# Value products of two quads of heads issued together in the attention stage of a two-layer decoder trunk

## The chip, the cores and the metric

The kernel runs on one core of a Trainium2 chip, in one launch. The metric is device time in microseconds (us); less is better. The kernel before took 1133.11 us, the median of three runs (1133.06 to 1133.26). One further execution was taken with the hardware profiler; all rows shown here come from it.

## The reference

Two layers of a hybrid decoder are computed for one sequence of 512 tokens with 1024 features, in float32. Layer 0 mixes tokens by a gated linear recurrence beside a short gated convolution; layer 1 mixes them by sliding-window attention. Each layer then has a mixture of 16 experts (two of one group for each token) and a gated per-layer embedding. The part that this case is about is the attention of layer 1: 16 query heads of width 64 over 2 key/value heads, a window of 128 keys, a learned sink for each head.

```
s = einsum('bnqkgd,bnskd->bkgnqs', q, kk) * scale        # scores, 128 queries x 256 keys for a block and head
s = where(mask, s, -inf)                                  # band of 128 keys
m = maximum(max(s, axis=-1), sink)
e = exp(s - m)
probs = e / (sum(e, axis=-1) + exp(sink - m))
o = einsum('bkgnqs,bnskd->bnqkgd', probs, vv)             # the value products
return o.reshape(bsz, t, D_MODEL) @ w_out + b_out
```

Everything else (the recurrence, the experts, the norms) is computed before and after this and is the same in both kernels.

## The kernel before

The program is written by hand, engine by engine, in one block for each engine; each engine works through its own list in order, and semaphores join them. There is no scheduler: the order in the code is the order on the chip. Large matrix products split each float32 operand into a high and a low part and take three products (`dense`). ScalarE (ACT) makes the high parts (`whi`, `ahi`), VectorE (DVE) the low ones (`wlo`, `alo`).

Attention is worked through in 16 quads. A quad is four heads of one block of 128 queries: quad w belongs to query block w // 4. For a quad the steps are these.

- `score(w)`, TensorE (PE): four matmuls of 64 rows each into the PSUM banks 4 and 5 (even quads) or 6 and 7 (odd quads). It raises `t_s`. In the profile these are the matmuls `psum<-arena` of shape 64*128.
- `mask_max(w, j)`, DVE, L2653 and L2659: a small copy and four mask-and-maximum instructions. Each of the four raises `t_neg`.
- `probs(u)`, ACT, L1870: four exponentials (u counts half quads, 0 to 31). Each raises `t_e`.
- `normalise(w)`, DVE, L2669 and L2672: one reciprocal and four scalings. Each scaling raises `t_prob`.
- `prob_T(u)`, PE, L1306: four transposes for a half quad into PSUM bank 2 or 3. It raises `t_pT`.
- `pT_copy(u)`, ACT, in the profile L1383 `arena<-psum`: a copy of the transposed probabilities out of PSUM. It raises `t_pTc`. The copies of a quad go to one of two buffers (`probs_T(w)`, chosen by w % 2), so from quad 2 on the copy waits for the value products of two quads earlier.
- `values(w)`, PE: four matmuls (two for quads 0 to 3, whose first key block is empty) into half of PSUM bank 0 or 1. It raises `t_pv`. In the profile these are the matmuls `psum<-arena` of shape 128*64.
- `o_hi(hb)`, ACT, L1383 `ahi<-psum`, and `o_lo(hb)`, DVE, L2678: the two parts of the output of two quads (hb = w // 2), after both their value products. `o_lo` raises `t_lo`.

The profile shows each float32 matmul of these steps as two records, so a quad's scores are x8 and its value products x8 (x4 for quads 0 to 3). The line of all matmuls that go through the helper is L569.

The waits that matter for the copy are written in ACT's block:

```
def pT_copy(u):
    w, j = u // 2, u % 2
    act.wait_ge(t_pT, u + 2)
    if w >= 2:
        act.wait_ge(t_pv, w - 1)
```

The order in the main loop, w from 0 to 15, is: on PE `prob_T(2w)`, `prob_T(2w + 1)`, `score(w + 3)`, `values(w - 1)`; on ACT `probs` of quad w + 1, `pT_copy(2w)`, `pT_copy(2w + 1)`, and in odd turns from 3 on `o_hi(w // 2 - 1)`; on DVE `mask_max` of quad w + 2, `normalise(w + 1)`, and in odd turns from 3 on `o_lo(w // 2 - 1)`. A "turn w" below is one pass of this loop, and "copy 2w" is `pT_copy(2w)`. After the loop come the value products of quad 15 and the output projection, a `dense` of 128x512 matmuls on PE, whose weights were loaded earlier.

Of the kernel before, what the change touches and what calls it, by code (L numbers as in the profile page):

```python
# [134 lines left out]
def build(nc, gm0, consts, hconsts, aconsts, gains, bout, x, pT, w_dense, w_moe, w_proj, out,  # L135
# [6 lines left out]
    with ctx:  # L142
# [237 lines left out]
        def first_key(n):  # L380

            return P if n == 0 else 0
# [5 lines left out]
        def probs_T(w):  # L388

            return area(AR_PTT, 2, 2, 512)[:, w % 2]  # L390
# [176 lines left out]
        def _(pe):  # L567
            def mm(o, l, r, start, stop, **kw):
                return nc.tensor.matmul(o, l, r, start=start, stop=stop, **kw)  # L569
# [686 lines left out]
            for q in range(2):  # L1256
                bank_read(BLK["akv"], q)
                o = PS[q][:, :]
                for kt in range(KT):
                    w = slice(kt * 256 + q * P, kt * 256 + (q + 1) * P)  # L1260
# [20 lines left out]
            def score(w):  # L1281


                n = w // 4
                if w < 4:
                    pe.wait_ge(t_q, (5, 5, 7, 9)[w])
                if w >= 2:
                    pe.wait_ge(t_neg, 4 * (w - 1))
                for j in range(2):
                    for hh in range(2):  # L1290
                        r = slice(64 * hh, 64 * hh + 64)
                        o = PS[4 + w % 2 * 2 + hh]
                        last = mm(o[:, j * KEYS + first_key(n):(j + 1) * KEYS],
                                  QT[r, 2 * (w % 4) + j, n * P:(n + 1) * P],
                                  KTa[r, n * P + first_key(n):(n + 2) * P], True, True)
                last.then_inc(t_s, 1)

            def prob_T(u):
                w, j = u // 2, u % 2
                pe.wait_ge(t_prob, 2 * u + 2)  # L1300
                if u >= 2:
                    pe.wait_ge(t_pTc, u - 1)
                for hh in range(2):
                    for kb in range(first_key(w // 4) // P, 2):
                        at = (hh * 2 + kb) * P
                        last = nc.tensor.transpose(  # L1306
                            PS[2 + j][:, at:at + P],
                            soft(w)[:, 2 * j + hh, kb * P:(kb + 1) * P], ident)
                last.then_inc(t_pT, 1)

            def values(w):


                n, hb = w // 4, w // 2
                pe.wait_ge(t_pTc, 2 * w + 2)
                if w % 2 == 0 and hb >= 2:
                    pe.wait_ge(t_lo, hb - 1)
                first = first_key(n) // P
                o = PS[hb % 2][:, w % 2 * 256:(w % 2 + 1) * 256]
                for kb in range(first, 2):  # L1320
                    for hh in range(2):
                        r = slice(64 * hh, 64 * hh + 64)
                        at = (hh * 2 + kb) * P
                        last = mm(o[r, :].rearrange("p (a b) -> p a b", a=2),
                                  VN[:, n + kb, hh * HD:(hh + 1) * HD],
                                  probs_T(w)[:, :, at:at + P], kb == first, kb == 1)
                last.then_inc(t_pv, 1)
# [12 lines left out]
            for w in range(QUADS):  # L1340
                prob_T(2 * w)
                prob_T(2 * w + 1)
                if w + 3 < QUADS:
                    score(w + 3)
                if w >= 1:
                    values(w - 1)
            values(QUADS - 1)

# [1570 lines left out]
```

## Time and profile before

| what | value |
|---|---|
| median of three runs | 1133.11 us |
| the profiled execution, its own time | 1134.14 us |
| its span in the profile | 1131.9 us |
| PE busy | 1107.4 us (98%) |
| DVE busy | 894.3 us (79%) |
| ACT busy | 749.9 us (66%) |
| mean granted TensorE clock | 0.998 of full speed |
| attention loop | about 663.5 to 710.2 us of the span |

The span is the time from the first to the last instruction in the profile; the execution's own time is 2.24 us longer, and this execution took 1.03 us more than the median. Busy time is a union of an engine's instructions. A row of the timeline gives the start, the length, the engine, the line and the operation with its operands; in square brackets stands the idle time before it, where there is one, and who ended it. Groups of equal instructions are merged into one row with a count.

### The profile page before, as it was taken

To read this page: it belongs to the slowest core of one execution; us is meant where nothing else is said; L and a number is where in the kernel's file an instruction comes from. 1 tells how busy PE (TensorE), PEld (TensorE's weight loads), DVE (VectorE), ACT (ScalarE), POOL (GpSimd) and SP (SyncE) were. 2 spreads that over 40 slices of the span, in tenths; PEclk is the share of its full clock that TensorE was granted. 3 is DMA by queue.
4 is the path that set the end of the run, shared out by engine and by line. 5 is a ranking of instruction groups with operands and counts; after the bars stand their busy time and mean duration, and the time that the engine had idled before them with its cause. 6 is when DMAs were issued, how large, how long until landed. Compare 5 with 4: busy or idle time off the path is not lost.

```text
span 1131.9 us, 16852 instructions
## 1 busy us (share of the span) xinstructions
PE 1107.4 (98%) x5722; PEld 886.0 (78%) x5722; DVE 894.3 (79%) x1226; ACT 749.9 (66%) x957; POOL 131.2 (12%) x91
## 2 busy tenths in 40 slices
PE   9999999999999999999999999999999999999996
PEld 7888878757888888888788866776888888888785
DVE  6483777368999999998966479637999999999886
ACT  7483322347878787788565469436787878787765
POOL 0000000011212212120000000001221212221000
PEclk9999999999999999999999999999999999999999
DMA  9473213336999999998851210433999999999632
GB/s 368 171 279 149 94 47 135 154 120 245 358 390 372 383 372 386 377 377 348 324 202 44 106 38 20 168 112 138 339 366 384 377 386 373 391 371 382 262 136 75
DMA packets 50595, 286.28 MB, mean 253 GB/s; under 512 B 9321, under 2 KB 9597, under 8 KB 21358
## 3 DMA queue, kind: packets, MB, share of 16 engines
q1 hardware_dynamic: 37086, 250.93, 57.6%
q0 software_dynamic: 13456, 34.65, 8.3%
q8 instruction: 33, 0.54, 0.2%
q14 instruction: 20, 0.16, 0.0%
HBM read 271.38 MB, written 30.41 MB: 267 GB/s over the span
## 4 chain that ended last, share of the span: by engine, by line
PE 86%; DVE 7%; ACT 4%; issue 1%; DMA 1%; ACTq 0%; DVEq 0%; POOLq 0%
PE psum L569 81%; PE psum L938 2%; DVE arena L2659 2%; ACT whi L1383 2%; DMA arena<-vscr,cur 1%; DVE arena L2672 1%; PE psum L979 1%; DVE wlo L1942 1%; PE psum L849 1%; ACT ahi L1383 1%; DVE h L2493 0%; DVE h L2500 0%; DVE wlo L1938 0%; DVE h L2486 0%; PE psum L655 0%
## 5 line engine op out<-in xcount | busy, mean ns | idle before, releaser
L1938 DVE TENSOR_TENSOR wlo<-raw,whi 128x2048 fp32r<-128x2048 f32 x200 | 456.1, 2289 | 69.8 <-ACT whi L1383 59.5
L569 PE MATMUL psum<-whi,ahi 128*128 128x512 f32 x1088 | 433.6, 400 | 2.7 <-ACT ahi L1383 2.1
L569 PE MATMUL psum<-wlo,ahi 128*128 128x512 f32 x1088 | 422.8, 390 | 0.8 <-DVE wlo L1942 0.8
L569 PE MATMUL psum<-whi,alo 128*128 128x512 f32 x1088 | 418.3, 391 | 0.0
L1383 ACT ACTIVATE whi<-raw 128x2048 fp32r<-128x2048 f32 x200 | 382.8, 1916 | 41.7 <-PE psum L569 41.7
L569 PEld LDWEIGHTS psum<-whi,ahi 128*128 128x128 f32 x1088 | 204.3, 188 | 49.2 <-issue 4.5
L569 PEld LDWEIGHTS psum<-whi,alo 128*128 128x128 f32 x1088 | 204.2, 188 | 43.7
L569 PEld LDWEIGHTS psum<-wlo,ahi 128*128 128x128 f32 x1088 | 204.5, 188 | 40.0 <-DVE wlo L1942 1.2
L1383 ACT ACTIVATE arena<-psum 128x512 f32<-128x512 f32 (+3 forms) x150 | 83.3, 565 | 109.0 <-PE psum L569 77.9
L1383 ACT ACTIVATE ahi<-psum 128x512 fp32r<-128x512 f32 x146 | 81.8, 594 | 102.8 <-PE psum L938 39.3
L2767 POOL DMA_INDIRECT arena<-vscr,cur x32 | 69.5, 2172 | 386.1 <-DVE cur L2379 370.9
L569 PE MATMUL psum<-ahi,whi 128*128 128x512 f32 x240 | 95.4, 398 | 1.1 <-DVE wlo L1942 1.1
L569 PE MATMUL psum<-ahi,wlo 128*128 128x512 f32 x240 | 93.6, 390 | 0.0
L569 PE MATMUL psum<-alo,whi 128*128 128x512 f32 x240 | 93.5, 389 | 0.0
L569 PE MATMUL psum<-arena 128*64 128x256 f32 (+10 forms) x762 | 89.0, 319 | 0.9 <-ACT arena L1383 0.8
L569 PEld LDWEIGHTS psum<-arena 128*128 128x128 f32 (+5 forms) x762 | 54.7, 151 | 29.0 <-issue 15.6
L2775 POOL DMA_INDIRECT yscr<-arena,cur x30 | 45.0, 1500 | 89.1 <-ACT arena L1383 86.3
L569 PEld LDWEIGHTS psum<-ahi,whi 128*128 128x128 f32 x240 | 45.1, 188 | 11.7 <-DVE wlo L1942 1.6
L569 PEld LDWEIGHTS psum<-ahi,wlo 128*128 128x128 f32 x240 | 45.0, 188 | 9.6
L569 PEld LDWEIGHTS psum<-alo,whi 128*128 128x128 f32 x240 | 45.1, 188 | 9.2 <-issue 0.2
L1942 DVE SCALAR_TENSOR_TENSOR wlo<-raw,arena,whi 128x512 fp32r<-128x512 f32 x48 | 32.8, 745 | 17.9 <-ACT whi L1383 17.8
L2394 DVE TENSOR_TENSOR alo<-psum,ahi 128x512 fp32r<-128x512 f32 x64 | 40.9, 679 | 3.9 <-ACT ahi L1383 3.9
(222 smaller groups left out, 894.5 us busy)
## 6 DMA issues: line engine op xcount, KB each, us to landing
raw<-w_moe_dram SPq DMA_DIRECT2D x192, 1024.0 KB, 8.8
raw<-w_dense_dram SPq DMA_DIRECT2D x34, 1024.0 KB, 8.8
yscr<-arena POOLq DMA_DIRECT2D x2, 4096.0 KB, 24.3
arena<-yscr SPq DMA_DIRECT2D x6, 1024.0 KB, 6.8
vscr<-arena POOLq DMA_DIRECT2D x8, 512.0 KB, 2.9
h<-x_dram SPq DMA_DIRECT2D x4, 512.0 KB, 7.5
arena<-w_proj_dram POOLq DMA_DIRECT2D x2, 1024.0 KB, 6.9
arena<-yscr SPq DMA_DIRECT2D x4, 512.0 KB, 4.4
```

What stands on the lines that cost most here:

```text
L569: return nc.tensor.matmul(o, l, r, start=start, stop=stop, **kw)
L849: last = nc.tensor.transpose(PS[4 + half][:, t * P:(t + 1) * P], h[:, tb, kt * P:(kt + 1) * P], ident)
L938: last = nc.tensor.transpose(PS[4 + half][:, t * P:(t + 1) * P], area(AR_XGS[par], D)[:, kt * P:(kt + 1) * P], ident)
L979: last = nc.tensor.transpose(PS[6][:, t * P:(t + 1) * P], area(AR_HID, 512)[:, t * P:(t + 1) * P], ident)
L1383: return nc.scalar.activation(o, i, ACT.Copy, scale=scale)
L1938: tt(wlo[:, b % SPL, :], raw[:, b % RAW, :], halves(whi[:, b % SPL, :]), ALU.subtract).then_inc(lo_ready, 1)
L1942: last = stt(wlo[:, b % SPL, w], raw[:, b % RAW, w], g, halves(whi[:, b % SPL, w]), ALU.mult, ALU.subtract)
L2394: tt(alo[w], PS[4 + half][:, :].rearrange("p (a b) -> p a b", a=4), halves(ahi[w]), ALU.subtract).then_inc(m["xlo"], 1)
L2659: nc.vector.tensor_tensor_reduce(out=soft(w)[:, 2 * j + hh, a:KEYS], in0=PS[4 + w % 2 * 2 + hh][:, j * KEYS + a:(j + 1) * KEYS], in1=mk[:, ...
L2672: ts(pr, pr, rden[:, k:k + 1], None, ALU.mult).then_inc(t_prob, 1)
L2767: nc.gpsimd.indirect_dma_start(out=area(AR_XGS[par], D), out_offset=None, in_=vscr[layer], in_offset=bass.IndirectOffsetOnAxis(ap=cur[:, p ...
L2775: nc.gpsimd.indirect_dma_start(out=yscr[layer], out_offset=bass.IndirectOffsetOnAxis(ap=cur[:, 2 + par:3 + par], axis=0), in_=area(AR_OUTS ...
```

## The change

In the PE loop, the value products are no longer issued in each turn. In an odd turn w the products of quad w - 2 and of quad w - 1 are issued one behind the other, behind the scores of quad w + 3. In an even turn none are issued. In turn 1 only quad 0 is there. ACT's, DVE's and all other lists stay as they are, and so do all waits.

```
                 prob_T(2 * w + 1)
                 if w + 3 < QUADS:
                     score(w + 3)
-                if w >= 1:
+                if w % 2 == 1:
+                    if w >= 2:
+                        values(w - 2)
                     values(w - 1)
             values(QUADS - 1)
```

The order on PE in the turns 6 and 7, before. L1306 are the transposes, L569 128x256 the scores, L569 64x256 the value products; the first eight rows that are no transposes belong, two by two, to the scores of quad 9, the values of quad 5, the scores of quad 10 and the values of quad 6.

```order
L569 MATMUL psum<-arena 128x256 [waits t_neg]
L569 MATMUL psum<-arena 128x256 x3
L569 MATMUL psum<-arena 64x256 [waits t_pTc]
L569 MATMUL psum<-arena 64x256 x3
L1306 MATMUL psum<-con,arena 128x128 [waits t_pTc,t_prob]
L1306 MATMUL psum<-con,arena 128x128 x3
L1306 MATMUL psum<-con,arena 128x128 [waits t_pTc,t_prob]
L1306 MATMUL psum<-con,arena 128x128 x3
L569 MATMUL psum<-arena 128x256 [waits t_neg]
L569 MATMUL psum<-arena 128x256 x3
L569 MATMUL psum<-arena 64x256 [waits t_lo,t_pTc]
L569 MATMUL psum<-arena 64x256 x3
```

The same place in the changed kernel, from the scores of quad 9 on:

```order
L569 MATMUL psum<-arena 128x256 [waits t_neg]
L569 MATMUL psum<-arena 128x256 x3
L1306 MATMUL psum<-con,arena 128x128 [waits t_pTc,t_prob]
L1306 MATMUL psum<-con,arena 128x128 x3
L1306 MATMUL psum<-con,arena 128x128 [waits t_pTc,t_prob]
L1306 MATMUL psum<-con,arena 128x128 x3
L569 MATMUL psum<-arena 128x256 [waits t_neg]
L569 MATMUL psum<-arena 128x256 x3
L569 MATMUL psum<-arena 64x256 [waits t_pTc]
L569 MATMUL psum<-arena 64x256 x3
L569 MATMUL psum<-arena 64x256 [waits t_lo,t_pTc]
L569 MATMUL psum<-arena 64x256 x3
```

The values of quad 5 have moved behind the transposes of quad 7 and the scores of quad 10.

The second place is the end of the loop on PE, turn 15, before. The rows are the transposes of quad 15, the values of quads 14 and 15, and the first matmul of the output projection.

```order
L1306 MATMUL psum<-con,arena 128x128 [waits t_pTc,t_prob]
L1306 MATMUL psum<-con,arena 128x128 x3
L1306 MATMUL psum<-con,arena 128x128 [waits t_pTc,t_prob]
L1306 MATMUL psum<-con,arena 128x128 x3
L569 MATMUL psum<-arena 64x256 [waits t_lo,t_pTc]
L569 MATMUL psum<-arena 64x256 x3
L569 MATMUL psum<-arena 64x256 [waits t_pTc]
L569 MATMUL psum<-arena 64x256 x3
L569 MATMUL psum<-whi,ahi 128x512 [waits t_pTc,t_lo,lo_ready]
```

And in the changed kernel, from the second half of these transposes on:

```order
L1306 MATMUL psum<-con,arena 128x128 [waits t_pTc,t_prob]
L1306 MATMUL psum<-con,arena 128x128 x3
L569 MATMUL psum<-arena 64x256 [waits t_pTc]
L569 MATMUL psum<-arena 64x256 x3
L569 MATMUL psum<-arena 64x256 [waits t_lo,t_pTc]
L569 MATMUL psum<-arena 64x256 x3
L569 MATMUL psum<-arena 64x256 [waits t_pTc]
L569 MATMUL psum<-arena 64x256 x3
L569 MATMUL psum<-whi,ahi 128x512 [waits t_pTc,t_lo,lo_ready]
```

The values of quad 13 now stand behind all transposes of quad 15, with those of quads 14 and 15 behind them.

## Rows read from the trace of the kernel before

**Rows 1.** Busy time of PE, PEld, DVE, ACT, POOL; then PEclk, DMA share, GB/s.

```profile
684.19:690.69 6.50, 6.36 (x52) 4.04 (x50) 6.43 (x32) 6.50 (x22) 0.00 (x0) 1.00 0.00 0
```

**Rows 2.** Chain of waits: start, us, engine and line.

```profile
699.57 1.61 DVE arena L2659 x8
...
708.43 23.88 PE psum L569 x112
```

**Rows 3.** Waits of PE in the loop: us in total, times, longest.

```profile
PEld psum L1306 <- DVE arena L2672: 8.8, 15, 1.2
```

**Rows 4.** Timeline of turns 9 to 12: DVE, PE and ACT.

```profile
692.31 0.68 DVE L2678 TENSOR_TENSOR alo<-psum,ahi 128x512 fp32r<-128x512 f32 x1
...
692.98 0.47 DVE L2659 CUSTOM_DVE_ANT_0 arena<-psum,arena 128x256 f32<-128x256 f32 x1
...
694.80 1.14 DVE L2672 TENSOR_SCALAR arena<-arena 128x256 f32<-128x256 f32 x4
...
695.48 1.18 PE L1306 MATMUL psum<-con,arena 128*128 128x128 f32 x8
...
696.17 1.12 ACT L1383 ACTIVATE arena<-psum 128x512 f32<-128x512 f32 x2
...
696.59 2.15 PE L569 MATMUL psum<-arena 64*128 64x256 f32 x16
...
697.19 0.59 ACT L1383 ACTIVATE ahi<-psum 128x512 fp32r<-128x512 f32 x1
...
699.64 1.07 ACT L1383 ACTIVATE arena<-psum 128x512 f32<-128x512 f32 x2
```

**Rows 5.** Timeline: turn 3, and the copies of turns 5, 7 and 9.

```profile
670.20 0.66 ACT L1383 ACTIVATE arena<-psum 128x256 f32<-128x256 f32 x2
...
670.36 1.72 PE L569 MATMUL psum<-arena 64*128 64x256 f32 x12
...
670.75 0.59 ACT L1383 ACTIVATE ahi<-psum 128x512 fp32r<-128x512 f32 x1
...
676.67 1.12 ACT L1383 ACTIVATE arena<-psum 128x512 f32<-128x512 f32 x2 [0.43 <-PE psum L1306]
...
683.17 1.12 ACT L1383 ACTIVATE arena<-psum 128x512 f32<-128x512 f32 x2
...
689.67 1.12 ACT L1383 ACTIVATE arena<-psum 128x512 f32<-128x512 f32 x2
```

**Rows 6.** Timeline from turn 13 to the output projection.

```profile
702.76 1.12 ACT L1383 ACTIVATE arena<-psum 128x512 f32<-128x512 f32 x2
...
703.17 1.08 PE L569 MATMUL psum<-arena 128*64 128x256 f32 x8
...
703.78 0.59 ACT L1383 ACTIVATE ahi<-psum 128x512 fp32r<-128x512 f32 x1
...
707.25 1.18 PE L1306 MATMUL psum<-con,arena 128*128 128x128 f32 x8
...
707.94 1.12 ACT L1383 ACTIVATE arena<-psum 128x512 f32<-128x512 f32 x2 [0.65 <-PE psum L1306]
...
708.36 1.95 PE L569 MATMUL psum<-arena 128*64 128x256 f32 x16
...
710.24 0.50 PE L569 MATMUL psum<-whi,ahi 128*128 128x512 f32 x1
...
710.36 0.60 ACT L1383 ACTIVATE ahi<-psum 128x512 fp32r<-128x512 f32 x1 [0.80 <-PE psum L569]
...
710.99 0.69 DVE L2678 TENSOR_TENSOR alo<-psum,ahi 128x512 fp32r<-128x512 f32 x1 [0.71 <-ACT ahi L1383]
```

**Rows 7.** Weight load in turn 11 behind the scores; columns as in rows 4.

```profile
697.65 0.63 PEld L569 LDWEIGHTS psum<-arena 128*64 128x64 f32 x8 [0.33 <-ACT arena L1383]
```

**Rows 8.** Busy time by engine and granted clock at the program's end; columns as in rows 1.

```profile
1122.00:1126.00 4.00, 1.18 (x6) 0.64 (x4) 1.93 (x5) 3.82 (x5) 0.00 (x0) 1.00 0.94 349
1126.00:1131.00 5.00, 0.00 (x0) 0.00 (x0) 2.21 (x5) 1.67 (x4) 0.00 (x0) 0.57 0.37 141
```

More of the change, by code:

```diff
@@ L1344, in _ @@
                     score(w + 3)
-                if w >= 1:
+                if w % 2 == 1:
+                    if w >= 2:
+                        values(w - 2)
                     values(w - 1)
```

## The prediction

> **What bounds the kernel now.** PE is busy 98% of the whole span, but the change touches one stage, so I read that stage. First the chain of waits: inside the attention loop it does not run over PE. It steps from DVE group to DVE group, and only from 708.43 on is it PE again, with the output projection [rows 2]. Then the busy time of one pair of turns (an even and an odd one), a stretch of 6.50 us between two `o_hi`: ACT is busy 6.50 of 6.50 us, DVE 6.43, PE 6.36, and the DMA share is 0.00 [rows 1]. So ACT and DVE have no slack, and a pair of turns costs 6.50 us because ACT's list is that long. PE's 6.36 us overstate it: its weight loads for the transposes wait 15 times for DVE's scalings, 8.8 us in all [rows 3]. PE works in the gaps the other two leave. What the reader is to see: a delay of ACT or DVE in this loop costs its full length, a change in PE's work costs only what it makes them wait.
>
> Last the timeline of one odd turn, 11 [rows 4]. DVE's scalings start at 694.80, the transposes at 695.48, ACT's first copy at 696.17, before the scores at 696.59 begin. The copy needs the products of quad 9 too (`t_pv`), but these were issued in turn 10, long before, so this wait costs nothing today.
>
> **The change part by part.** No instruction is added or removed; all 16 calls of `values` are moved or stay. Moved are those of the odd quads 1, 3, ..., 13: each goes from an even turn to the next odd one, behind eight transposes and the scores. Seven copies wait for exactly these products: copy 2w with w = 3, 5, ..., 15 waits for quad w - 2. Behind each of these copies ACT has its partner copy, `o_hi` and then the next exponentials, and DVE's `o_lo` waits for `o_hi`. No DMA is issued in this loop by SP or in PE's list, no queue is passed, and the even quads keep their place or stand 1 us later behind their partner, where only `o_hi` needs them (it stands behind two copies of 1.12 us that wait longer).
>
> What the wait costs the first time: in turn 3 the scores of quad 6 start at 670.36 with the products behind them, together x12 and 1.72 us, which is what would stand there now too (eight score records, four of a short quad) [rows 5]. The products end at 672.08. From a product's end to ACT it takes 0.05 us: 708.36 + 1.95 = 710.31 against `o_hi` at 710.36 [rows 6]. So copy 6 starts at 672.13 instead of 670.20 [rows 5]: 1.93 us late.
>
> From there a loop closes that was not closed before, and its length sets the pace. From one waiting copy to the next:
> 1. copy to `o_hi`: 697.19 - 696.17 = 1.02 [rows 4]; in turn 3 the copies are short, 670.75 - 670.20 = 0.55 [rows 5]
> 2. `o_hi` to `o_lo`: 710.99 - 710.36 = 0.63 [rows 6]
> 3. `o_lo` to the masks of the next quad: 692.98 - 692.31 = 0.67 [rows 4]
> 4. masks to scalings: 694.80 - 692.98 = 1.82 [rows 4]
> 5. scalings to transposes: 695.48 - 694.80 = 0.68 [rows 4]
> 6. transposes to scores: 696.59 - 695.48 = 1.11 [rows 4]
> 7. scores and the products behind them, to the release: 2.15 + 0.05 = 2.20 [rows 4]; with a short quad behind them 1.72 + 0.05 = 1.77 [rows 5]; without scores 1.08 + 0.05 = 1.13 [rows 6]
>
> Sum: 1.02 + 0.63 + 0.67 + 1.82 + 0.68 + 1.11 + 2.20 = 8.13 us for a pair, against 6.50. Each full pair adds 1.63 us. The scalings also need ACT's four exponentials, which stand between `o_hi` and the next copies: 699.64 - 697.19 = 2.45 us for `o_hi` and these four [rows 4]. They are ready 1.02 + 2.45 = 3.5 us behind the waiting copy, and the scalings come at 1.02 + 0.63 + 0.67 + 1.82 = 4.14. They fit.
>
> Now turn by turn, the start of the waiting copy, new against old:
> - turn 3: 672.13 against 670.20, +1.93
> - turn 5: 0.55 + 0.63 + 0.67 + 1.82 + 0.68 + 1.11 + 1.77 = 7.23 on, 679.36 against 676.67, +2.69 [rows 5]
> - turn 7: 8.13 on, 687.49 against 683.17, +4.32 [rows 5]
> - turn 9: 695.62 against 689.67, +5.95 [rows 5]
> - turn 11: 703.75 against 696.17, +7.58 [rows 4]
> - turn 13: no scores are left, 8.13 - 2.20 + 1.13 = 7.06 on, 710.81 against 702.76, +8.05 [rows 6]
> - turn 15: no masks are left. 1.02 to `o_hi`, then 707.25 - 703.78 = 3.47 to the transposes (over the last exponentials), 708.36 - 707.25 = 1.11, and 1.13 for the products of quad 13: 6.73 on, 717.54 against 707.94, +9.60 [rows 6]
>
> The end: the products of quad 15 need the second copy, 717.54 + 1.12 = 718.66. By then PE is done with quad 14 (two products take 1.95 us, from 716.41 to 718.36). From the start of the last products to the output projection it is 1.88 / 2 = 0.94, where 1.88 = 710.24 - 708.36 [rows 6]. So the projection starts near 719.6 instead of 710.24: +9.4 us.
>
> Behind it everything moves as one piece. The DMA queues stand still in the loop (share 0.00 [rows 1]), the weights of the next stages are in their buffers, and loads resume when these are used; nothing there is nearer to the loop's old end than to its new one. On the profiled execution this gives 1131.9 + 9.4 = 1141.3 us of span and 1134.14 + 9.4 = 1143.5 us of time. The profiled execution lay 1.03 us over the median of the runs, so a median of **1142.5 us** is predicted.
>
> Bounds of what the trace does not show. A product that ACT waits for behind scores is shown nowhere: from below it comes 697.65 - 696.59 = 1.06 (scores) [rows 4, 7] plus 0.94 (one of two products) [rows 6] = 2.00 behind the scores' start, from above at 2.15 + 0.63 (step 2, the longest such hand-over here); I take 2.20, next to the observed end of the products. The lower end takes 0.2 off six times, the upper adds 0.6 six times: -1.2 and +3.5 us. Steps 1 to 6 were seen with engines that were full; each may be 0.05 us off, over some 35 steps that is 1.7 us either way. If the even turn's copies or the second half's transposes have some slack that my chain charges, the turns 13 and 15 lose most, up to 2 us.
>
> **A rule of the Trainium skill.** In turn 11 the weight load of the products has 0.33 us before it behind the scores [rows 7], which I take as the price of a change of matmul kind. "TensorEngine Tiling (Array Packing)" of the Trainium skill, section "Key Properties", says that a change of the tiling mode drains TensorE; by it scores (64*128), products (128*64) and transposes (128*128) each cost a drain, and the change has five switches in a pair of turns instead of six. By that rule alone the time would fall; the size and what it is worth are the second rival below.
>
> **The rivals.**
>
> *The late products cost once, not in each pair.* If ACT or DVE could catch up between two waits, only the last turn would count: transposes at 707.25, products of quad 13 until 709.49, copy at 709.49 instead of 707.94, +1.55; a chain that catches up half of each pair's 1.63 gives 1.93 + 0.76 + 3 x 0.82 + 0.24 + 0.78 = 6.2 less the 0.2 at the end. Times: 1134.7 to 1139. Against it speaks that ACT is busy 6.50 of 6.50 and DVE 6.43 [rows 1]. For it, that DVE sat only on part of the chain's waits and rounding may hide 0.1 us here and there.
>
> *PE's switches are the bound (faster).* Where PE's issue of three kinds of matmul sets the pace, one gap of 0.33 us goes in each of seven even turns: 7 x 0.33 = 2.3 us, 1130.8 us. It decides as soon as PE does not wait for DVE before its transposes. Against it: PE's loads do wait there, 15 times, 8.8 us [rows 3], over 0.5 us each time; a gap of 0.33 us taken out only lengthens that wait. This is the side of a gain, and it needs the copies not to wait for the moved products, which the code excludes.
>
> *Every wait adds in full.* If the transposes kept their distance from ACT's list and not from DVE's, each of seven copies would come 696.59 + 2.20 - 696.17 = 2.62 us late on top of a full ACT: 7 x 2.5 = 17.5 us, 1150.6 us. Against it: the transposes hang on the scalings, and these on masks and exponentials that begin before the wait ends.
>
> *The clock falls.* With pairs of 8.13 us PE is busy 6.36 / 8.13 = 78%. If the granted clock went to 1.2 GHz there, steps 6 and 7 (3.3 us) would take twice as long, five to six times: 17 to 20 us more, about 1161 us. The trace speaks against it: the clock is 1.00 (2.4 GHz) even in 4 us with 1.18 us of PE work, and falls to 0.57 only where PE does nothing for 5 us [rows 8].
>
> **How the numbers follow.** What this kernel's measurement can tell from no change is about 0.2%, 2.3 us. Chances: the closed loop as worked out 76% (own range 1140 to 1145); catching up, 12%, of which a third stays under +2.3 us; full addition 5%; the clock 2%; PE's switches 2%; nothing measurable for another reason 3%. Slower is then 76 + 8 + 5 + 2 = 91%, the same 4 + 3 = 7%, faster 2%. The likeliest is 1142.5. For 8 in 10 the closed loop is taken with the upper part of the catching up: 1139 to 1145.5.
>
> **What the changed kernel's profile would show.** ACT's row for the copies in the odd turns gets idle time before it, released by PE's L569 and not by L1306: about 1.6 us in each full pair, some 11 us in all with the ends. DVE's `o_lo` (L2678) waits for `ahi` in each odd turn, where it now does so only twice. The pair of turns is 8.1 us long in the middle of the loop, PE's matmul counts are the same, the clock stays at 1.00, and behind the output projection all stages keep their lengths. If the pair stays at 6.5 us, step 7 or the reading that ACT is full is wrong. If it is 9 us, the exponentials and not `o_lo` carry the chain. If the loop is 8.1 us and the total is not up by nine, something behind it gives time back.

## The result and the profile after

The changed kernel takes 1147.75 us, the median of four runs (1146.49 to 1149.23), against 1133.18 us for the kernel before: a ratio of 1.0127 with a 95% interval of 1.0113 to 1.0142, 14.6 us slower. The prediction said 1142.5 us and a range up to 1145.5: slower was right, the size was not. The four runs also spread over 2.7 us, where the kernel before spreads over 0.3 in four runs (over 1.3 and 1.8 us in the fifteen and twenty runs taken of it for the experiments). The clock in their records goes with it: 0.995 at 1146.49 us, 0.994 at 1147.33, 0.992 at 1148.17 and 1149.23.

The page of the profile shows the first sign in section 2. Part 1 and the granted clock by slices:

```profile
span 1145.1 us, 16852 instructions
...
PE 1110.5 (97%) x5722; PEld 888.0 (78%) x5722; DVE 895.2 (78%) x1226; ACT 749.8 (65%) x957; POOL 131.6 (11%) x91
...
PEclk9999999999999999999999998999999999999999
```

The counts are those of before. The busy time of ACT and DVE is within 1 us of before; PE's has grown by 3.1 us with the same instructions, and one slice has an 8 in the clock row, where the kernel before had a 9.

The waits of the stretch 660 to 722 us (us in total, times, longest), where before the transposes' loads waited 8.8 us [rows 3]:

```profile
PEld psum L1306 <- DVE arena L2674: 16.0, 11, 2.3
ACT arena L1385 <- PE psum L569: 15.1, 7, 3.7
PE psum L1306 <- DVE arena L2674: 11.9, 8, 1.9
DVE alo L2680 <- ACT ahi L1385: 9.2, 6, 3.1
```

The second row is the predicted wait: seven copies on ACT wait for PE's L569, the products, and the fourth is DVE's `o_lo` behind them. Predicted were some 11 us for the copies, not 15.1.

The timeline at the same places as [rows 4 to 6], ACT's waiting copies of the turns 3, 5, 7, 9, 11, 13 and 15, with PE and DVE in turn 7 and PE's transposes and first projection matmul later on:

```profile
671.98 0.66 ACT L1385 ACTIVATE arena<-psum 128x256 f32<-128x256 f32 x2 [1.90 <-PE psum L569]
...
679.27 1.09 ACT L1385 ACTIVATE arena<-psum 128x512 f32<-128x512 f32 x2 [1.26 <-PE psum L569]
...
684.05 1.18 PE L1306 MATMUL psum<-con,arena 128*128 128x128 f32 x8 [1.86 <-DVE arena L2674]
...
685.16 3.01 PE L569 MATMUL psum<-arena 64*128 64x256 f32 x24
...
687.41 1.09 ACT L1385 ACTIVATE arena<-psum 128x512 f32<-128x512 f32 x2 [1.69 <-PE psum L569]
...
689.02 0.69 DVE L2680 TENSOR_TENSOR alo<-psum,ahi 128x512 fp32r<-128x512 f32 x1 [1.55 <-ACT ahi L1385]
...
695.57 1.09 ACT L1385 ACTIVATE arena<-psum 128x512 f32<-128x512 f32 x2 [1.70 <-PE psum L569]
...
700.35 1.64 PE L1306 MATMUL psum<-con,arena 128*128 128x128 f32 x8 [1.86 <-DVE arena L2674]
...
705.28 1.09 ACT L1385 ACTIVATE arena<-psum 128x512 f32<-128x512 f32 x2 [3.25 <-PE psum L569]
...
713.26 1.08 ACT L1385 ACTIVATE arena<-psum 128x512 f32<-128x512 f32 x2 [1.52 <-PE psum L569]
...
717.70 1.78 PE L1306 MATMUL psum<-con,arena 128*128 128x128 f32 x8 [1.92 <-DVE arena L2674]
...
721.49 1.08 ACT L1385 ACTIVATE arena<-psum 128x512 f32<-128x512 f32 x2 [3.74 <-PE psum L569]
...
723.64 0.50 PE L569 MATMUL psum<-whi,ahi 128*128 128x512 f32 x1
```

The loop begins 0.21 us earlier in this span than in that of before (the first transposes stand at 663.35 and not 663.56), so 0.21 is added for a comparison. Turn 5 then has its copy at 679.48 (predicted 679.36), turn 7 at 687.62 (687.49), turn 9 at 695.78 (695.62). A pair is 687.41 - 679.27 = 8.14 and 695.57 - 687.41 = 8.16 us long; 8.13 was predicted. Up to here the forecast holds to 0.2 us. The next pair is 705.28 - 695.57 = 9.71 us. Its transposes start as far behind the last copy as before (4.78 us), but last 1.64 instead of 1.18, and the copy waits 3.25 instead of 1.70. The same stretch by engines, with three more (columns as in [rows 1]):

```profile
690.00:692.00 2.00, 0.34 (x4) 0.00 (x0) 1.97 (x11) 2.00 (x7) 0.00 (x0) 1.00 0.00 0
...
700.00:704.00 4.00, 3.65 (x18) 2.40 (x20) 3.73 (x18) 2.02 (x9) 0.00 (x0) 0.61 0.00 0
...
710.00:714.00 4.00, 3.94 (x22) 2.53 (x24) 3.45 (x17) 2.48 (x10) 0.00 (x0) 0.64 0.33 129
...
718.00:722.00 4.00, 4.00 (x24) 2.60 (x22) 0.17 (x1) 0.51 (x2) 0.00 (x0) 0.58 0.00 0
```

The column behind POOL's is the granted clock, as a mean over the row: 1.00 is 2.4 GHz, and a value such as 0.61 is a stretch that ran partly at 2.4 and partly at 1.2 GHz. The clock fell three times, each time within 1.1 us after PE had taken up its work again behind a gap like that of the first row, and it was still down when ACT came to wait for PE. The gap of the first row itself was followed by no fall. The projection starts at 723.85 instead of 710.24, 13.6 us late, of which 9.4 were predicted. Behind it nothing changes: the step into the experts waits for the same DMA at 809.75 instead of 796.35, with the 0.21 again 13.6 us later. From profiled run to profiled run the times differ by 1147.33 - 1134.14 = 13.2 us; the medians differ by 1.4 more, since the profiled execution of before was 1.0 slower than its median and that of the changed kernel 0.4 faster.

### The profile page after: what moved, and what is told of

It reads as the page before. It is cut to its first block, busy times and chain, and to the rows that moved or that the text cites. A ratio compares the mean times of both kernels' runs of the same rounds, so it can differ in the third digit from the quotient of the medians.

```text
span 1145.1 us, 16852 instructions
## 1 busy us (share of the span) xinstructions
PE 1110.5 (97%) x5722; PEld 888.0 (78%) x5722; DVE 895.2 (78%) x1226; ACT 749.8 (65%) x957; POOL 131.6 (11%) x91
## 4 chain that ended last, share of the span: by engine, by line
PE 86%; DVE 6%; ACT 4%; DMA 2%; issue 2%; SPq 0%; ACTq 0%; DVEq 0%; POOLq 0%
PE psum L569 80%; PE psum L938 2%; DMA arena<-vscr,cur 1%; ACT whi L1385 1%; PE psum L979 1%; DVE arena L2661 1%; ACT ahi L1385 1%; PE psum L1306 1%; DVE wlo L1944 1%; DMA h<-x_dram 1%; ACT arena L1385 1%; PE psum L849 1%; DVE h L2495 0%; DVE arena L2674 0%; DVE h L2502 0%
## 5 line engine op out<-in xcount | busy, mean ns | idle before, releaser
L569 PE MATMUL psum<-whi,ahi 128*128 128x512 f32 x1088 | 433.5, 400 | 2.6 <-ACT ahi L1385 2.1
L569 PE MATMUL psum<-wlo,ahi 128*128 128x512 f32 x1088 | 422.9, 390 | 0.8 <-DVE wlo L1944 0.8
L569 PE MATMUL psum<-whi,alo 128*128 128x512 f32 x1088 | 418.2, 391 | 0.0
L569 PEld LDWEIGHTS psum<-whi,ahi 128*128 128x128 f32 x1088 | 204.3, 188 | 49.2 <-issue 4.4
L569 PEld LDWEIGHTS psum<-whi,alo 128*128 128x128 f32 x1088 | 204.2, 188 | 43.6
L569 PEld LDWEIGHTS psum<-wlo,ahi 128*128 128x128 f32 x1088 | 204.5, 188 | 40.3 <-DVE wlo L1944 1.2
L569 PE MATMUL psum<-ahi,whi 128*128 128x512 f32 x240 | 95.4, 398 | 1.1 <-DVE wlo L1944 1.1
L569 PE MATMUL psum<-ahi,wlo 128*128 128x512 f32 x240 | 93.6, 390 | 0.0
L569 PE MATMUL psum<-alo,whi 128*128 128x512 f32 x240 | 93.5, 390 | 0.0
L569 PE MATMUL psum<-arena 32*128 32x128 f32 (+10 forms) x762 | 91.7, 329 | 1.3 <-ACT arena L1385 1.1
L569 PEld LDWEIGHTS psum<-arena 128*128 128x128 f32 (+5 forms) x762 | 57.0, 156 | 30.4 <-issue 18.7
L569 PEld LDWEIGHTS psum<-ahi,whi 128*128 128x128 f32 x240 | 45.0, 188 | 11.7 <-DVE wlo L1944 1.6
L569 PEld LDWEIGHTS psum<-ahi,wlo 128*128 128x128 f32 x240 | 45.1, 188 | 9.5
L569 PEld LDWEIGHTS psum<-alo,whi 128*128 128x128 f32 x240 | 45.1, 188 | 9.2 <-issue 0.2
```

## The experiments

Theory A: the loop over the late products costs the 9.4 us worked out, and the rest is the granted clock, which fell because PE stood still for 1.9 us in each pair. Theory B: the rest lies in other waits of the loop. Each run is timed beside the kernel before on its own chip; that took 1133.93 us in the first four and 1133.55 us in the last four.

**PE's gap filled.** The changed kernel, with the scores of the odd quads 5 to 15 computed twice (`EXTRA = 4`), and as many spare matmuls in turn 14.

```
+EXTRA = 4
...
-                for j in range(2):
-                    for hh in range(2):
+                extra = EXTRA if w % 2 == 1 and w >= 5 else 0
+                pairs = [(j, hh) for j in range(2) for hh in range(2)]
+                for j, hh in pairs + pairs[:extra]:
+                    if True:
...
+                if w == 14:
+                    pe.wait_ge(t_neg, 4 * QUADS)
+                    for i in range(EXTRA):
+                        mm(PS[6 + i % 2][:, 0:KEYS], QT[0:64, 0, 0:P],
+                           KTa[0:64, 0:KEYS], True, True)
```

> The changed kernel with extra work for PE where it idles: the scores of the odd quads 5 to 15 (issued in even turns) are computed twice, into the same place with the same result, and four matmuls into unused PSUM stand at the end of turn 14. Each fills 1.06 us of the 1.9 us in which PE waits for the scalings. Theory (the closed loop costs 9.4 us, and the other 5 us are the granted clock, which fell because PE stood still for 1.9 us in each pair): the pair of turns stays at 8.15 us, the clock stays at 1.00, the time is 1142.5 us (1141.5 to 1143.5) and its spread is under 0.5 us. Rival (the 5 us lie in the loop's own waits or behind the loop): the time stays near 1147.7 us whatever the clock does, or rises by the added 6.4 us of PE work.

Measured: 1143.53 us (1143.00 to 1143.98), 9.6 us over before, ratio 1.0085 (1.0070 to 1.0100). With more work for PE the kernel took 4.2 us less than the changed kernel's 1147.75 us, and 5.0 us less when each is set against the kernel before as timed beside it (9.6 against 14.6 us). The spread is 1.0 us, not under 0.5. ACT's copies of the turns 9 to 15, the projection, and the clock where it had fallen:

```profile
695.44 1.09 ACT L1393 ACTIVATE arena<-psum 128x512 f32<-128x512 f32 x2 [1.69 <-PE psum L570]
...
703.59 1.09 ACT L1393 ACTIVATE arena<-psum 128x512 f32<-128x512 f32 x2 [1.69 <-PE psum L570]
...
710.67 1.08 ACT L1393 ACTIVATE arena<-psum 128x512 f32<-128x512 f32 x2 [0.63 <-PE psum L570]
...
717.41 1.09 ACT L1393 ACTIVATE arena<-psum 128x512 f32<-128x512 f32 x2 [2.24 <-PE psum L570]
...
719.56 0.50 PE L570 MATMUL psum<-whi,ahi 128*128 128x512 f32 x1
```

```profile
700.00:704.00 4.00, 3.78 (x32) 2.59 (x32) 3.61 (x17) 2.31 (x9) 0.00 (x0) 1.00 0.02 4
...
710.00:714.00 4.00, 4.00 (x29) 2.89 (x26) 2.45 (x10) 3.37 (x12) 0.00 (x0) 1.00 0.21 85
```

The steps are 8.15, 7.08, 6.74 and 2.15 us; predicted were 8.13, 7.06, 6.73 and 2.06. In the changed kernel they were 9.71, 7.98, 8.23 and 2.15: the three falls of the clock cost 1.56 + 0.90 + 1.49 = 3.95 us in the profiled run. PE's longest wait before transposes is 1.0 us here, against 1.9. Theory A holds, and B is out: ACT's waits and the pair of 8.15 us are as they were while the clock was up, and only the falls are gone. Filling the gap makes it shorter and PE busier at once, so the run does not tell which of the two kept the clock up.

**Half of the filling** (`EXTRA = 2`).

> As fill4, with half of the extra work: two more matmuls (0.53 us) in each even turn from 2 on, PE's wait is left at 1.3 us in each pair. Theory: the pair stays at 8.15 us; the clock is steadier than in the changed kernel, 1142.5 us if 1.3 us of standing still is short enough, something up to 1146 us if not. Rival: 1147.7 us as before, since half the idle time is still there.

Measured: 1144.07 us (1143.05 to 1144.13), 10.1 us over before, ratio 1.0086 (1.0070 to 1.0101). In the profiled run PE stood still for 1.26 and then four times for 1.42 or 1.43 us before the transposes (not the 1.3 expected), with the clock at 1.00 behind all five. It fell behind the next gap, that of turn 15:

```profile
714.95 1.18 PE L1309 MATMUL psum<-con,arena 128*128 128x128 f32 x8 [1.52 <-DVE arena L2682]
```

```profile
716.00:718.00 2.00, 2.00 (x12) 1.19 (x12) 0.00 (x0) 0.00 (x0) 0.00 (x0) 0.55 0.00 0
```

The last two steps are 7.54 and 2.44 instead of 6.74 and 2.15: a fall worth 1.1 us. Half of the filling keeps most of the clock.

**The products of two quads ahead of the scores.**

```
                 prob_T(2 * w + 1)
-                if w + 3 < QUADS:
-                    score(w + 3)
                 if w % 2 == 1:
                     if w >= 2:
                         values(w - 2)
                     values(w - 1)
+                if w + 3 < QUADS:
+                    score(w + 3)
```

> The value products of two quads still go together in odd turns, but ahead of the scores of quad w + 3 and not behind them. Theory of the closed loop: the release comes 1.13 us behind the transposes and not 2.20, the loop is 8.13 - 1.07 = 7.06 us against ACT's own 6.50; by turns the copies are late by about 0.8, 0.8, 1.3, 1.9, 2.5, 2.9, 4.4 us, the projection by 4.3 us: 1137.4 us (1136.5 to 1138.5), clock 1.00 since PE's wait shrinks to about 1 us. Rival (grouping itself costs, by drains or by the copies of two quads that collide, and not the place behind the scores): near 1142 us or more, as in the changed kernel.

Measured: 1139.76 us (1139.10 to 1141.30), 5.8 us over before, ratio 1.0053 (1.0038 to 1.0069). The waiting copies of the turns 7 and 9, PE's transposes of turn 15 and the projection:

```profile
685.48 1.08 ACT L1385 ACTIVATE arena<-psum 128x512 f32<-128x512 f32 x2 [0.63 <-PE psum L569]
...
692.56 1.08 ACT L1385 ACTIVATE arena<-psum 128x512 f32<-128x512 f32 x2 [0.63 <-PE psum L569]
...
711.17 1.18 PE L1306 MATMUL psum<-con,arena 128*128 128x128 f32 x8 [2.58 <-DVE arena L2674]
...
715.62 0.50 PE L569 MATMUL psum<-whi,ahi 128*128 128x512 f32 x1
```

The pair is 7.08 us (7.06 expected) and the projection 4.9 us late (4.3 expected; the loop begins 0.47 later in this span, which is taken off). The total missed by 1.5 us, of which 0.6 is in the loop's ends; the other 0.9 stays open, though in the profiled run 0.47 of it stand ahead of the loop, where the order is the same. The clock was 1.00 in the profiled run's loop, also behind the gap of 2.58 us; the run at 1141.30 had a clock of 0.995. The grouping is the same here as in the changed kernel, and the price is 5.8 us instead of 9.6 (with the clock up in both): the place behind the scores costs the other 3.8. What is left I put down to the place behind the transposes of turn w, for which the copy still waits; no run tries it alone.

**One late product.** The order of before, with quad 7's products in turn 9 (`LATE = (9,)`).

```
+LATE = (9,)
...
-                if w >= 1:
+                if w in LATE:
+                    values(w - 2)
+                if w >= 1 and w + 1 not in LATE:
+                    values(w - 1)
```

> The order of the kernel before in all turns but one: the products of quad 7 go from turn 8 to turn 9, behind the scores of quad 12. The copy of turn 9 then starts at 690.09 + 2.20 = 692.29 instead of 689.67, 2.6 us late. Theory: ACT is full, so a single late copy is never caught up: 1133.2 + 2.6 = 1135.8 us (1135.3 to 1136.2). Rival (a single wait is caught up, in part or in full, since only the loop over DVE, 1.63 us a pair, is truly on the path): 1134.8 us or less, down to 1133.2.

Measured: 1135.70 us (1135.35 to 1137.08), 1.8 us over before, ratio 1.0016 (1.0007 to 1.0025). ACT's copies of the turns 9, 11, 13 and 15:

```profile
693.01 1.09 ACT L1386 ACTIVATE arena<-psum 128x512 f32<-128x512 f32 x2 [2.68 <-PE psum L570]
...
699.36 1.07 ACT L1386 ACTIVATE arena<-psum 128x512 f32<-128x512 f32 x2
...
705.69 1.08 ACT L1386 ACTIVATE arena<-psum 128x512 f32<-128x512 f32 x2
...
710.84 1.12 ACT L1386 ACTIVATE arena<-psum 128x512 f32<-128x512 f32 x2 [0.65 <-PE psum L1307]
```

The copy comes 2.68 us late, as expected (the loop begins 0.66 later in this span). But then the pairs are 6.35 and 6.33 us long, where the kernel before has 6.50 and 6.59, and at the projection 2.23 us are left. So ACT had 0.15 to 0.26 us of slack in a pair that its 6.50 of 6.50 busy us hid, and the theory that a late copy is never caught up is wrong by that much (1.8 us over before by the medians, 2.6 expected). ACT's copies run as fast as PE's transposes let them, x2 in 1.12 us where it waits within and 1.07 where it does not.

**Late products in three turns** (`LATE = (7, 9, 11)`).

> Late products in the turns 7, 9 and 11 only (quads 5, 7 and 9 behind the scores), all else as in the kernel before. Theory: the first late copy costs 2.62 us, each further one closes the loop and adds 8.13 - 6.50 = 1.63: copies late by 2.6, 4.3 and 5.9 us; as in the run with one late copy about 0.5 us comes back: 5.4 us over the kernel before, clock 1.00 or one short fall. Rival (each costs in full): 7.9 us. Rival (the first costs 1.6 like the others): 4.4 us or less.

Measured: 1142.42 us, 8.9 over before, ratio 1.0070 (1.0053 to 1.0087), but in two kinds: one run at 1139.18 with a clock of 0.997, 5.6 us over before as expected, and three at 1142.09 to 1142.95 with 0.994. The profiled run is one of the latter, and its pairs are 9.69 and 9.73 us:

```profile
690.49 1.83 PE L1307 MATMUL psum<-con,arena 128*128 128x128 f32 x8 [1.86 <-DVE arena L2675]
...
700.18 1.48 PE L1307 MATMUL psum<-con,arena 128*128 128x128 f32 x8 [1.86 <-DVE arena L2675]
```

```profile
692.00:696.00 4.00, 4.00 (x26) 2.25 (x24) 1.87 (x9) 0.76 (x4) 0.00 (x0) 0.74 0.00 0
...
700.00:704.00 4.00, 3.82 (x18) 2.45 (x20) 3.56 (x17) 1.84 (x8) 0.00 (x0) 0.61 0.00 0
```

PE stood still before the transposes for 1.86 us twice, at 690.49 and 700.18 us; the clock fell behind the first of these already, and behind both. In the run at 1139.18 us the record shows no such loss.

**A third buffer.** The changed kernel with three buffers for the transposed probabilities, so that the copy waits for the products of quad w - 3.

```
-            return area(AR_PTT, 2, 2, 512)[:, w % 2]
+            if w % 3 == 2:
+                return ar[:, 9728:9728 + 5120 + 512][:, 0:5632].rearrange(
+                    "p (a b) -> p a b", b=512)[:, 0:11:10, :]
+            return area(AR_PTT, 2, 2, 512)[:, w % 3]
...
-                if w >= 2:
-                    act.wait_ge(t_pv, w - 1)
+                if w >= 3:
+                    act.wait_ge(t_pv, w - 2)
```

The move of the small table (`AR_ST2`) is not shown.

> The changed kernel with three buffers for the copied probabilities instead of two (the third lies in free columns of the arena, and a small table of statistics has moved). The copy of turn w then waits for the products of quad w - 3, issued a turn or two before: the wait that the change created is gone, but o_hi in odd turns still needs the products of quad w - 2 behind the scores. Theory (the same loop, now closed over o_hi and not over the copy): it is 1.02 us shorter, 0.63 + 0.67 + 1.82 + 0.68 + 1.11 + 2.20 = 7.11 us a pair against 6.50; ACT's wait stands before o_hi; the projection starts some 4.1 us later than before: 4 to 5 us over the kernel before. Rival (the copies alone held it up): within 1 us of the kernel before.

Measured: 1137.08 us (1136.76 to 1139.86), 3.5 us over before, ratio 1.0042 (1.0028 to 1.0056): a little less than the 4 to 5 expected. Three of the five runs lie at 1136.76 to 1137.08 us with a clock of 0.997, two at 1139.52 and 1139.86 with 0.996. ACT, the turns 7 and 9:

```profile
683.79 1.07 ACT L1388 ACTIVATE arena<-psum 128x512 f32<-128x512 f32 x2
685.52 0.60 ACT L1388 ACTIVATE ahi<-psum 128x512 fp32r<-128x512 f32 x1 [0.66 <-PE psum L572]
...
690.91 1.06 ACT L1388 ACTIVATE arena<-psum 128x512 f32<-128x512 f32 x2
...
692.63 0.60 ACT L1388 ACTIVATE ahi<-psum 128x512 fp32r<-128x512 f32 x1 [0.66 <-PE psum L572]
```

The copies no longer wait, the wait stands before `o_hi`, and the pair is 692.63 - 685.52 = 7.11 us, as expected. The projection comes 3.6 us late (713.42 - 710.24, and 0.45 since the loop begins that much earlier in this span).

**The third buffer, and `o_hi` and `o_lo` a turn later.**

```
-                if w >= 3 and w % 2 == 1:
-                    o_hi(w // 2 - 1)
+                if w >= 4 and w % 2 == 0:
+                    o_hi(w // 2 - 2)
+            o_hi(2 * TB - 2)
             o_hi(2 * TB - 1)
```

and the same for `o_lo`.

> As buf3, and o_hi and o_lo stand one turn later (in even turns from 4 on), so that they too find the products done. The products still go in twos behind the scores. Theory (the order on PE costs nothing where nobody waits for it): the pair is back at 6.3 to 6.5 us, the time is that of the kernel before, within 1 us; the clock stays up. Rivals: grouping in itself costs (the time stays 2 us or more above the kernel before), or one change of matmul kind fewer in each pair gains up to 2.3 us.

Measured: 1134.09 us (1133.26 to 1134.94), ratio 1.0006 (0.9997 to 1.0016): no difference from the kernel before, with the products still in twos behind the scores. In the profiled run the pair is 6.50 us (copies at 686.61, 693.11 and 699.61) and the clock in the loop 1.00. Nobody waits for the products in the loop, and the 14.6 us are gone; only at the projection, where the last products are waited for, 0.6 us are left (710.84 against 710.24).

**The same with PE's order of the kernel before.**

> The three buffers and the later o_hi and o_lo of buf3late, with PE's order of the kernel before (the products of one quad in each turn). It tells what the buffers do by themselves. Theory: the kernel before's time within 0.5 us, perhaps 0.5 to 1 us less, since the pair was 6.33 us long in the one-late-copy run where ACT ran without any wait, against 6.50. Rival: buf3late is faster than this one by more than 1 us, if fewer changes of matmul kind are worth anything.

Measured: 1133.49 us (1132.51 to 1134.09), ratio 0.9999 (0.9990 to 1.0009). The third buffer gains nothing in the old order: the pair stays at 6.50 to 6.51 us, since each copy there follows PE's transposes, and these DVE. The hope for 0.5 to 1 us was wrong. Beside it, the run above with one change of matmul kind fewer in a pair is 0.6 us slower, within the two intervals. No version beat the kernel before.

## Why the prediction was right and where it was wrong

- *What bounds the stage.* Right that PE does not, and that a delay of ACT or DVE counts. The reading "ACT has no slack" was 0.15 to 0.26 us a pair off (one late product). The chain of waits, which went over DVE [rows 2], was the better guide than the 6.50 of 6.50.
- *The late copies and the closed loop.* Right. In the changed kernel, before the clock fell, the copies came within 0.16 us of the numbers worked out; with the gap filled, all steps of the loop and its ends did within 0.09 us, and the projection was 9.7 us late (719.56 + 0.34 for the start of that span, less 710.24) against 9.4. The three variants of the loop confirm its terms: without the scores before the release 7.08 us, without the copies in it 7.11, and no measurable cost where the loop is opened altogether.
- *Behind the loop everything moves as one piece.* Right, 13.6 us at the projection and 13.6 us at the experts' DMA.
- *The rival of the clock.* This step failed: the sum holds the clock at 1.00 throughout, so its fall is a term put at nothing, and it measured 3.95 us in the profiled run (5.0 us by the medians with the gap filled). The loop's 9.4 us were right (9.7 with the gap filled), and 9.7 + 3.95 makes the 13.6 us at the projection. I gave the fall 2%, because the clock was 1.00 in 4 us with only 1.18 us of PE work [rows 8]. That row shows one stretch, in which PE is busy up to 1123.2 us and then has no more work, at the end of a long busy time. It says nothing on a gap of 1.9 us that comes back every 8 us, and no row of the kernel before had such gaps: the loop I had worked out created them, 8.13 - 6.36 us of standing still a pair, and I did not treat this as a new condition. The range should have reached to it. Its price was off the other way: I charged every pair at half speed, 17 to 20 us, while the clock fell three times, and in part, at a price of 4 us in the profiled run and, by its time, an estimated 6 in the slowest.
- *The other rivals.* Catching up once (12%) is out but for the 0.45 us of the run with one late product. Full addition (5%) is out: it would have made each pair some 2.5 us longer, and the pairs with the clock up are 8.14 to 8.16 us, 1.65 longer than before. The one run of three late products with the clock up agrees, 5.6 us and not 7.9. The rule of "TensorEngine Tiling (Array Packing)" of the Trainium skill, section "Key Properties", that a change of the mode drains TensorE, speaks for a gain. I had priced it at up to 2.3 us from the 0.33 us of [rows 7]; where the grouped order was tried with no one waiting for it, it gained nothing (1134.09 against 1133.49 us). The drains may exist; in this loop, where PE waits for DVE, they are worth nothing that these runs can measure.

## What to carry to other kernels

Before an instruction is moved later, list the instructions on other engines that need it and follow each around until it comes back: if the way back is a loop, the sum of its steps is the new pace, and it is not the sum of the waits. A product that frees a buffer is as urgent as the buffer is scarce; one more buffer, and the consumers moved with it, makes the same order free. Where a change makes TensorE wait regularly, count a fall of its clock among the costs, unless the trace shows the clock under gaps of that length and rhythm.

## What the runs showed of the hardware

I had not expected the clock to fall with PE busy for 77% of the time (6.29 of 8.15 us in the pair from 692.20 to 700.35 us of the changed kernel, all of it at 1.00 and right ahead of the first fall). It went to 1.2 GHz behind gaps of 1.9 us: in the changed kernel's profiled run behind the last three of six gaps (1.70 to 1.92 us) and not behind the first three, and with only two such gaps in the whole loop (late products in three turns) the time and the mean clock show a fall in three runs of four. With gaps of 1.0 us in each pair it stayed at 1.00. The length of a gap alone does not decide: in other profiled runs the clock fell behind one of 1.52 us (half of the filling) and stayed at 1.00 behind a single one of 2.58 us (products ahead of the scores) and of 1.90 us (third buffer). What decides is not shown by these runs.

With useless matmuls in the gaps the kernel took 1143.53 us against 1147.75 us. And the falls go with a wider spread: 2.7 us over four runs with them, 1.0 us with the gap filled; and in three of the other experiments (products ahead of the scores, late products in three turns, third buffer) the runs with a lower mean clock took some 1.5 us or more longer than those with a higher one.
